# The delta rule's matrix from unscaled keys, with the key-key products issued first

## What is computed

```python
k_beta = k * beta[..., None]
a_mat = jnp.where(strict, jnp.einsum('bhnid,bhnjd->bhnij', k_beta, k) * decay, 0.0)
lhs = a_mat + jnp.eye(C, dtype=f32)
rhs = jnp.concatenate([v * beta[..., None], k_beta * jnp.exp(g_cum)[..., None]], axis=-1)
sol = lax.linalg.triangular_solve(lhs, rhs, left_side=True, lower=True, unit_diagonal=True)
u, w = sol[..., :dv], sol[..., dv:]
qk = jnp.where(incl, jnp.einsum('bhnid,bhnjd->bhnij', q, k) * decay, 0.0)
# then chunk by chunk: v_new = u - w @ state; o = q_dec @ state + qk @ v_new; state = decayed state + k_dec^T @ v_new
```

## Time and profile before

| | us |
|---|---|
| median of 3 runs | 994.93 (994.51 to 995.14) |
| profiled execution, its own time | 1000.5 |
| its span | 998.5 |
| TensorE busy | 958.2 (96% of the span) |
| VectorE, ScalarE, GpSimd busy | 605.9, 458.6, 137.9 |
| mean granted clock of TensorE | 0.983 |

### The profile page before, as it was taken

The page is one execution under the profiler, slowest core; times in us unless marked ns, Lnnn a source line. Parts: engine busy times, 40 slices in busy tenths (PEclk is TensorE's granted clock), DMA queues, the critical chain, the costliest instruction groups (busy, mean ns, idle before and its releaser), DMA issues. The chain is left out here.

```text
span 998.5 us, 12382 instructions
## 1 busy us (share of the span) xinstructions
PE 958.2 (96%) x4951; PEld 810.1 (81%) x4951; DVE 605.9 (61%) x815; ACT 458.6 (46%) x664; POOL 137.9 (14%) x93
## 2 busy tenths in 40 slices
PE   5998999998999999999999999999999999999998
PEld 4787888877899788888888888988887788888886
DVE  3548878978624566565443574787775565554541
ACT  4454454862134355544333543564645354444531
POOL 4015322753521100000000000210000000000100
PEclk9999899997799999999999999999999999999999
DMA  9465352431200255555465764542453255554651
GB/s 269 156 215 167 113 161 93 141 127 44 84 1 1 85 169 169 173 186 189 169 189 191 274 198 120 190 155 98 130 177 116 85 169 186 194 173 122 231 204 70
DMA packets 76691, 149.31 MB, mean 150 GB/s; under 512 B 2768, under 2 KB 9088, under 8 KB 76512
## 3 DMA queue, kind: packets, MB, share of 16 engines
q1 hardware_dynamic: 75296, 144.06, 44.4%
q10 hardware_dynamic: 720, 3.66, 1.0%
q0 software_dynamic: 624, 0.87, 0.7%
HBM read 147.53 MB, written 1.05 MB: 149 GB/s over the span
## 5 line engine op out<-in xcount | busy, mean ns | idle before, releaser
L1407 DVE TENSOR_TENSOR w_lo<-raw,w_hi 128x2048 fp32r<-128x2048 f32 (+3 forms) x130 | 287.1, 2220 | 179.8 <-ACT w_hi L967 179.4
L429 PE MATMUL gemm<-w_hi,s_hi 128*128 128x512 f32 (+3 forms) x912 | 355.7, 390 | 14.5 <-DVE w_lo L1407 10.7
L430 PE MATMUL gemm<-w_lo,s_hi 128*128 128x512 f32 (+3 forms) x912 | 348.5, 382 | 0.0
L431 PE MATMUL gemm<-w_hi,s_lo 128*128 128x512 f32 (+3 forms) x912 | 348.3, 382 | 0.0
L967 ACT ACTIVATE w_hi<-raw 128x2048 fp32r<-128x2048 f32 (+3 forms) x142 | 259.1, 1837 | 172.3 <-DMA raw<-in_w_in_dram 51.1
L429 PEld LDWEIGHTS gemm<-w_hi,s_hi 128*128 128x128 f32 x912 | 173.3, 190 | 49.1 <-issue 11.9
L431 PEld LDWEIGHTS gemm<-w_hi,s_lo 128*128 128x128 f32 x912 | 173.1, 190 | 33.0
L430 PEld LDWEIGHTS gemm<-w_lo,s_hi 128*128 128x128 f32 x912 | 173.2, 190 | 31.1 <-issue 0.5
L2080 POOL TENSOR_TENSOR sm<-sm 128x2 f32<-128x2 f32 (+4 forms) x14 | 29.1, 2075 | 502.6 <-DVE sm L1451 307.7
L2074 POOL TENSOR_TENSOR w_lo<-raw,w_hi 128x2048 fp32r<-128x2048 f32 x12 | 55.8, 4662 | 195.9 <-ACT w_hi L967 195.9
L984 ACT ACTIVATE mix<-gemm,sm 128x512 f32<-128x512 f32 (+2 forms) x25 | 16.3, 653 | 74.9 <-PE gemm L431 74.9
(11 more groups left out here) (295 smaller groups left out, 995.0 us busy)
## 6 DMA issues: line engine op xcount, KB each, us to landing
raw<-in_w_in_dram SPq DMA_DIRECT2D x42, 1024.0 KB, 5.1
raw<-in_w_mlp_up_dram SPq DMA_DIRECT2D x16, 1024.0 KB, 5.5
raw<-in_w_mlp_down_dram SPq DMA_DIRECT2D x16, 1024.0 KB, 5.1
raw<-in_w_gate_dram SPq DMA_DIRECT2D x10, 1024.0 KB, 5.1
raw<-in_w_up_dram SPq DMA_DIRECT2D x10, 1024.0 KB, 5.1
raw<-in_w_down_dram SPq DMA_DIRECT2D x10, 1024.0 KB, 5.2
raw<-in_w_out_dram SPq DMA_DIRECT2D x8, 1024.0 KB, 5.0
raw<-in_w_xkv_dram SPq DMA_DIRECT2D x8, 1024.0 KB, 5.1
```

Of the source, the lines that this page charges most:

```text
L429: nc.tensor.matmul(o, hi, wh, start=kt == 0, stop=False)
L430: nc.tensor.matmul(o, hi, wl, start=False, stop=False)
L431: last = nc.tensor.matmul(o, lo, wh, start=False, stop=kt == blk["kt"] - 1)
L1407: V.tensor_tensor(w_lo[:, s, 0:kn, 0:width], raw[:, s, 0:kn, 0:width], w_hi[:, s, 0:kn, 0:width].bitcast(F32), ALU.subtract)\
```

## The change

VectorE no longer scales the keys before the key-key products, and TensorE no longer transposes scaled keys. Both kinds of products take YT as it is. `key_products` issues key-key first, then one quarter of B_Z, then key-query with a wait for the AT unit whose bank it takes. For the inverse to come out right, the factors go elsewhere: AT is multiplied by RNE (norm squared times beta) at eviction, VB by the ratio VRK (the inverse of the norm) on GpSimd, UV by BRK (norm times beta) at eviction, and KBG is the unscaled key times its decay. HBT, KB, KBT, the turning and ScalarE's copies go. QK moves to where KB was, XI and O1 to where QK was.

Order: on VectorE AT is evicted before the split of B_GA's first chunk, QK behind it, then the second chunk's split; the multiplication of z moves from behind QK to behind XI and XT. On TensorE the transposes of LT also wait for a QK unit, a quarter each of B_GA moves; on GpSimd KBG comes before KD, and VB's multiplication between the masks of level 0 and those of level 1.

```diff
-        XI = view(ar, 8368, 16, P)
+        XI = view(ar, 4272, 16, P)
@@ TensorE
+            def key_products(u, other, name):
+                for q in range(4):
+                    h, tok = 4 * (u % 2) + q, slice(P * (u // 2), P * (u // 2) + P)
+                    last = nc.tensor.matmul(M[(u + 2) % 4][:, P * q:P * q + P], YT[:, 8 + h, tok], YT[:, other + h, tok], start=True, stop=True)
+                last.then_inc(sem(name), 1)
...
-                for q in range(4):
-                    h, tok = 4 * (u % 2) + q, slice(P * (u // 2), P * (u // 2) + P)
-                    last = nc.tensor.matmul(M[(u + 2) % 4][:, P * q:P * q + P], YT[:, 8 + h, tok], YT[:, h, tok], start=True, stop=True)
-                last.then_inc(sem("gdn_kq"), 1)
+                key_products(u, 8, "gdn_kk")
             mm(B_Z + 1, quarters=[3])
+            for u in range(4):
+                pe.wait_ge(sem("gdn_at"), u + 1)
+                key_products(u, 0, "gdn_kq")
             mm(B_GA, quarters=[0])
-            pe.wait_ge(sem("gdn_kb"), 2)
-            for e in range(4):
-                pe.wait_ge(sem("gdn_qk"), e + 1)
-                for j in range(2):
-                    for t in range(NT):
-                        last = nc.tensor.transpose(M[(e + 2) % 4][:, (2 * j + t) * P:(2 * j + t + 1) * P], KB[:, t, 2 * e + j, :], ident)
-                last.then_inc(sem("gdn_ktT"), 1)
-            pe.wait_ge(sem("gdn_kt"), 4)
-            for u in range(4):
-                for q in range(4):
-                    last = nc.tensor.matmul(M[u][:, P * q:P * q + P], YT[:, 8 + h, tok], KBT[:, h, tok], start=True, stop=True)
-                last.then_inc(sem("gdn_kk"), 1)
-            mm(B_GA, quarters=[1, 2])
...
                 pe.wait_ge(sem("inv_lt"), u + 1)
+                pe.wait_ge(sem("gdn_qk"), (u + 2) % 4 + 1)
...
-            mm(B_GA, quarters=[3])
+            mm(B_GA, quarters=[1, 2])
...
                     unit(u, LT, XI, lv, 0).then_inc(sem("inv_p"), 1)
+                if lv == 1:
+                    mm(B_GA, quarters=[3])
...
+            pe.wait_ge(sem("gdn_vs"), 2)
@@ ScalarE
-            for e in range(4):
-                act.wait_ge(sem("gdn_ktT"), e + 1)
-                nc.scalar.activation(KBT[:, 2 * e:2 * e + 2, :], M[(e + 2) % 4].rearrange("p (a b) -> p a b", a=2), ACT.Copy).then_inc(sem("gdn_kt"), 1)
@@ VectorE
-            split(B_GA, 0)
...
+            link(V.tensor_tensor(VRK, SSK[:, 16:32], RQK[:, 16:32], ALU.mult))
             link(V.tensor_scalar(RQK, RQK, 0.5, None, ALU.mult))
             V.tensor_tensor(KDF, RQK[:, 16:24], ED[:, 0:8], ALU.mult).then_inc(sem("gdn_kdf"), 1)
             link(V.tensor_tensor(BRK, RQK[:, 16:32], BT, ALU.mult))
-            for t in range(NT):
-                V.tensor_tensor(KB[:, t], KN[:, t], spread(BRK[:, 8 * t:8 * t + 8], 2, P), ALU.mult).then_inc(sem("gdn_kb"), 1)
+            link(V.tensor_tensor(RNE, RQK[:, 16:32], BRK, ALU.mult))
...
+            for u in range(4):
+                dve.wait_ge(sem("gdn_kk"), u + 1)
+                decayed(AT, u, RNE, "gdn_at")
+            split(B_GA, 0)
...
             for u in range(4):
                 dve.wait_ge(sem("gdn_kq"), u + 1)
-                dve.wait_ge(sem("gdn_dme"), u + 1)
-                decayed(QK, M[(u + 2) % 4], u, "gdn_qk")
-            z_block(B_Z + 1, 1)
+                decayed(QK, u, RQK[:, 16:32], "gdn_qk")
             split(B_GA, 1)
-            for u in range(4):
-                dve.wait_ge(sem("gdn_kk"), u + 1)
-                decayed(AT, M[u], u, "gdn_at")
...
                 V.tensor_tensor(XT[:, n, :], eye, LT[:, n, :], ALU.subtract).then_inc(sem("inv_xt"), 1)
+            z_block(B_Z + 1, 1)
...
-                V.tensor_copy(UV[:, 0, 4 * half:4 * half + 4, :], M[2 + half].rearrange("p (a b) -> p a b", a=4)).then_inc(sem("gdn_uc"), 1)
+                V.tensor_tensor(UV[:, 0, 4 * half:4 * half + 4, :], M[2 + half].rearrange("p (a b) -> p a b", a=4),
+                                spread(BRK[:, 4 * half:4 * half + 4], 2, P), ALU.mult).then_inc(sem("gdn_uc"), 1)
@@ GpSimd
+            pool.wait_ge(sem("gdn_e"), 1)
+            pool.tensor_tensor(KBG, KN[:, 1], spread(EG[:, 8:16], 2, P), ALU.mult).then_inc(sem("gdn_kbg"), 1)
             pool.wait_ge(sem("gdn_kdf"), 1)
             pool.tensor_tensor(KD, KN[:, 0], spread(KDF, 2, P), ALU.mult).then_inc(sem("gdn_kd"), 1)
-            pool.wait_ge(sem("gdn_kb"), 2)
-            pool.tensor_tensor(KBG, KB[:, 1], spread(EG[:, 8:16], 2, P), ALU.mult).then_inc(sem("gdn_kbg"), 1)
...
-                        pool.wait_ge(sem("gdn_kk"), 4)
                         pool.wait_ge(sem("gdn_at"), u + 1)
...
+                if lv == 0:
+                    pool.wait_ge(sem("gdn_vb"), 4)
+                    for t in range(NT):
+                        pool.tensor_tensor(VB[:, t], VB[:, t], spread(VRK[:, 8 * t:8 * t + 8], 2, P), ALU.mult).then_inc(sem("gdn_vs"), 1)
```

More of the change, by code:

```diff
@@ L245, in build @@
         VB = view(ar, 6320, NT, 8, P)
-        KB = view(ar, 8368, NT, 8, P)
-        KBT = view(ar, 19632, 8, SEQ)
         KD = view(ar, 21680, 8, P)
@@ L250, in build @@
         AT = view(ar, 0, 16, P)
-        QK = view(ar, 4272, 16, P)
+        QK = view(ar, 8368, 16, P)
         LT = view(ar, 19632, 16, P)
         XT = view(ar, 17584, 16, P)
-        XI = view(ar, 8368, 16, P)
+        XI = view(ar, 4272, 16, P)
         PS = view(ar, 2048, 16, P)
@@ L258, in build @@
         ST = view(ar, 0, 8, P)
-        O1 = view(ar, 8368, NT, 8, P)
+        O1 = view(ar, 4272, NT, 8, P)
         def st(at, n):
@@ L270, in build @@
         NEGM, SUMS, RSUM = st(100, 32), st(132, 32), st(164, 32)
-        GA_, BT, HBT = st(196, 16), st(212, 16), st(516, 16)
+        GA_, BT = st(196, 16), st(212, 16)
         SP = st(228, 48)
@@ L275, in build @@
         KDF, BRK = st(372, 8), st(404, 16)
+        RNE, VRK = st(308, 16), st(324, 16)
         SSK, RQK = st(420, 32), st(452, 32)
@@ L1528, in _ @@
             link(V.tensor_scalar(BT, BT, 0.5, 0.5, ALU.mult, ALU.add))
-            V.tensor_scalar(HBT, BT, 0.5, None, ALU.mult)
             dve.wait_ge(sem("g_ln"), 1)
@@ L1661, in _ @@
                     h = 2 * (e - 12)
-                    f = HBT.rearrange("p (t h) -> p h t", t=2)[:, h:h + 2, :]
-                    sig(V.tensor_tensor(VB[:, :, h:h + 2, :].rearrange("p t j d -> p j t d"), M[3].rearrange("p (j t d) -> p j t d", j=2, t=2),
-                                        spread(f, 3, P), ALU.mult), "gdn_vb")
+                    sig(V.tensor_copy(VB[:, :, h:h + 2, :].rearrange("p t j d -> p j t d"), M[3].rearrange("p (j t d) -> p j t d", j=2, t=2)), "gdn_vb")
                 if e in (5, 9):
@@ L1687, in _, with decayed @@
             link(V.tensor_tensor(BRK, RQK[:, 16:32], BT, ALU.mult))
-            for t in range(NT):
-                V.tensor_tensor(KB[:, t], KN[:, t], spread(BRK[:, 8 * t:8 * t + 8], 2, P), ALU.mult).then_inc(sem("gdn_kb"), 1)
+            link(V.tensor_tensor(RNE, RQK[:, 16:32], BRK, ALU.mult))
+            def decayed(dst, u, factors, name):
+                bank = M[(u + 2) % 4]
+                dve.wait_ge(sem("gdn_dme"), u + 1)
+                for q in range(4):
+                    n = 4 * u + q
+                    ins = V.scalar_tensor_tensor(dst[:, n, :], bank[:, P * q:P * q + P], factors[:, n:n + 1], DM[:, n, :], ALU.mult, ALU.mult)
+                ins.then_inc(sem(name), 1)
+            for u in range(4):
+                dve.wait_ge(sem("gdn_kk"), u + 1)
+                decayed(AT, u, RNE, "gdn_at")
+            split(B_GA, 0)
             link(V.tensor_scalar(RQK[:, 0:16], RQK[:, 0:16], P ** -0.5, None, ALU.mult))
@@ L1693, in _ @@
             link(V.tensor_tensor(FQ.rearrange("p (t h) -> p t h", t=2), RQK[:, 0:16].rearrange("p (t h) -> p t h", t=2), spread(QRS, 2, 8), ALU.mult))
[L1695 to L1704, removed]
             for u in range(4):
                 dve.wait_ge(sem("gdn_kq"), u + 1)
-                dve.wait_ge(sem("gdn_dme"), u + 1)
-                decayed(QK, M[(u + 2) % 4], u, "gdn_qk")
-            z_block(B_Z + 1, 1)
+                decayed(QK, u, RQK[:, 16:32], "gdn_qk")
             split(B_GA, 1)
-            for u in range(4):
-                dve.wait_ge(sem("gdn_kk"), u + 1)
-                decayed(AT, M[u], u, "gdn_at")
             eye = spread(ident, 1, 4)
+            dve.wait_ge(sem("gdn_kd"), 1)
             dve.wait_ge(sem("gdn_kbg"), 1)
@@ L1741, in _ @@
                 if lv == 1:
+                    for t in range(NT):
+                        dve.wait_ge(sem(f"ev{t}"), B_Z + 2)
                     zg = ZG.rearrange("p t (h d) -> p (t h) d", d=P)
@@ L1749, in _ @@
                 dve.wait_ge(sem("gdn_u"), half + 1)
-                V.tensor_copy(UV[:, 0, 4 * half:4 * half + 4, :], M[2 + half].rearrange("p (a b) -> p a b", a=4)).then_inc(sem("gdn_uc"), 1)
+                V.tensor_tensor(UV[:, 0, 4 * half:4 * half + 4, :], M[2 + half].rearrange("p (a b) -> p a b", a=4),
```

(4 more changed lines are left out.)

## The result

The changed kernel takes 989.05 us (988.20 to 990.13, 4 runs) against 995.03 (994.51 to 996.43) for the kernel before on the same chip: ratio 0.9938, 95% interval 0.9921 to 0.9955. It is faster by 6.0 us, clear of noise, and less than half as much as forecast (13.0, to 981.9, with a range up to 987.2). Its profiled execution has a span of 987.8 us and a time of 989.75.

What follows compares the result with a forecast made beforehand. TensorE, busy 958.2 of 998.5 us, bounds the kernel. The ceiling of 17.7 less 3.0 of new idle leaves 14.6, less 1.6 for the clock gives 13.0: 994.9 - 13.0 = 981.9 us, range 978.4 to 987.2.

Steps and rivals of the forecast that it cites:

- the stage: First key product to level 2's first product on TensorE; 48.7 us before, 36.1 forecast.
- three gaps: TensorE idle before level 2: 2.39 us (VectorE's line 1699), 0.69 (ScalarE's turned keys), 2.31 (GpSimd's level 1 mask).
- the ceiling: Most the change can bring between the key products and level 2: 17.7 us, with 27.97 us of TensorE work remaining.
- the new wait: TensorE idle ahead of LT's transposes, waiting for QK units 3 and 4: 1.8 to 3.0 us.
- So they cost nothing: GpSimd's two VB multiplications, 1.90 us each ahead of level 1's masks: zero cost, up to 3.8 if uncovered.
- Case B: Mask 4 also passes before VectorE's short operations: QK evictions start at 234.3, TensorE idles 3.0 us ahead of LT's transposes.
- I take it as 0.2: RNE's short operation on VectorE passes KD on the shared path: 0.2 us, or 1.9 later if KD goes first.
- one low stretch of 3.2 us: Clock at 0.50 behind the idle at LT's transposes, half of 3.2 us lost: 1.6 us.
- since the saving is in fixed durations it is taken over in us: Final sum: the 13.0 us gain is subtracted unscaled from the median of 994.9, giving 981.9.
- the second small gap: Wait for QK unit 4 within LT's transposes, after the wait for unit 3: 0.6 us.
- the long low stretch: Rival 2: low clock for 7 to 10 us, gain 9.6 to 11, time 984 to 985.5; chance 0.20.
- The rival that PSUM evictions take turns with GpSimd: Rival 3: line 1699's 32 operations wait for GpSimd, price 10.8 us, time 1001; chance 0.03.

Runs made afterwards that it cites:

- the three moves: Changed kernel with RNE before KD's signal, q's norms' operations behind z's multiplication, and VB's multiplication behind level 2's masks: 979.49 us, ratio 0.9829.
- VB later: Changed kernel, but GpSimd multiplies VB behind the masks of level 2 instead of those of level 0: 985.70 us, ratio 0.9879.
- z undone: Changed kernel with z's multiplication again behind QK, ahead of the second split of B_GA: 988.14 us, ratio 0.9912.
- both moves inside level 1: Kernel before, turned keys kept, with z's multiplication behind XI and XT and the three operations on q's norms inside level 1: 988.74 us, ratio 0.9918.
- the dense quarter: Changed kernel, but one of the two quarters of B_GA behind LT's transposes stands ahead of them: 987.02 us, ratio 0.9906.

## Why the prediction was wrong

The reading of the stage held: which three gaps there were, that the two long low stretches hung on them, the ceiling (31.8 us reached of 31.5), key-query products without a wait, UV's evictions at no cost (1.28 us for a pair, before and after), no idle in level 1, and the place and releaser of the new wait. The direction was right, the size was not. What failed is the start of QK's evictions, which came 4.3 us later than forecast because VectorE's short operations stood behind GpSimd's long ones. The failed steps, of which the second weighs most:

- "So they cost nothing", of VB's multiplications. They were priced at zero. I looked for their cover only on GpSimd's side (is level 1's mask late?) and not for what queues behind them on the other engine. Moving them brought 3.3 us.
- The short operations between split and QK. Case B let "two such operations" pass and had QK start at 234.3; it started at 238.01, or 238.6 on the old kernel's time axis (the stage begins 0.61 later there). I had counted the wait for masks 3 and 4, but not that GpSimd has more work behind the masks, nor that the single-input operation waits. The three took 5.0 us where 2.8 was forecast. Moving them brought 6.9 us, the clock's part included.
- "I take it as 0.2", of RNE. The rows gave RNE no lead over KD, and a loss of 1.9 if it came second; KD went first in all five profiles of kernels with this order. A race that close should have been taken at its worse end. This wait is the cause of the 1.31 us ahead of B_GA and of at least 1.7 of QK's lateness, and moving RNE brought 3.6 us.
- The clock: one low stretch of 3.2 us was forecast for 3.0 us of idle. With 5.12 us of idle it was 6.8, which is some 1.8 us more lost.
- "since the saving is in fixed durations it is taken over in us", of the sum. Some 9.5 us of the ceiling were low clock, and the profiled execution had more of it than most: its time was 1000.5 and its mean clock 0.983, while executions of the same kernel that took 995 to 996 us show 0.986 to 0.988. At 990 us that is 3 to 5 us less lost to the lower level, which a median execution can't save. Which stretches it lacks is not shown.

The gains of the three moves overlap, so they can't be added: together they brought 9.6 us.

Put together for the stage, QK's unit is 4.3 us late, and the longer low stretch (1.8), less the second small gap that the wait hides (0.6), adds 1.2: 36.1 + 5.5 = 41.6 us, where 41.4 was measured. The times don't follow as closely. Between the two profiled executions the span fell by 10.7 us, of which 7.3 lie in the stage; of the other 3.4, half is the low stretch at 343.9, which the changed kernel's profile lacks. Between the medians it is 6.0 (4.5 to 7.9 by the interval), since the kernel before was profiled in an execution 5.5 us above its median, and the changed one 0.7 above.

Of the rivals, the long low stretch was the nearest, and its time of 984 to 987 was still too low. The rival that PSUM evictions take turns with GpSimd is refuted by 4.23 us for sixteen beside the masks.

The Trainium skill's GPSIMD Engine Reference (section Specifications) says that GpSimd contends with operations of VectorE that have two SBUF inputs or run in a 2-port mode. The trace agrees with the first half (1.82 and 1.93 us for 16 elements). For the second, VectorE's L1692 has one input and stood 1.26 us behind a mask; no view shows an operation's mode, so that it ran in such a mode is only likely. I had cited the second half, priced it at 1.3, and left it out of the sum.

What stays open: why the third short operation sometimes slips in between two of GpSimd's (0.16) and sometimes not (1.93), and how much of the scatter between executions it makes.

## What to carry to other kernels

An operation of 0.2 us costs what stands in front of it on the shared path: when a chain on VectorE is critical, put no SBUF-to-SBUF operation, however small, where GpSimd has a queue of long ones, and let VectorE finish its short ones before it signals GpSimd. When work moves to an idle engine, ask not only whether its results come in time but whom it blocks while it runs. And take one part of a change alone: here moving one multiplication gave as much as all of it, and the rest gave its 8 to 9 us only once the queues were in order. Last, read a profiled execution's clock beside that of the others before its low stretches are counted as a saving.

## What the runs showed of the hardware

- Idle TensorE time of the same size and place had different ends. Two pieces of 1.04 or 1.05 and 1.13 us stand ahead of the same dense matmuls (343.6 in the kernel before) in all twelve profiles. In five (the kernel before, VB later, z undone, both moves inside level 1, the dense quarter) some 3.4 us at the lower clock followed, in the other seven none, the changed kernel among them (the clock is 1.00 from 332.0 to 335.5 and after). So a price for such idle is a range, zero to 1.7 us here, and one profile doesn't settle it.
- One kernel's executions fell into two groups 7 us apart, with mean granted clocks of 0.990 to 0.993 and 0.983 to 0.986.
- A 16-element operation of VectorE with one SBUF input took 1.26 us, to the end of GpSimd's mask, where it takes 0.17 with GpSimd idle (1.26 or 1.27 in four more kernels that have it behind the split).
- Sixteen evictions of VectorE out of PSUM took 4.23 us beside GpSimd's masks, and 4.22 with GpSimd idle.
